# Eighteen of the last network's gate and up tile pairs as block products with seven multiplications, one weight sum added by a DMA

## The reference

```python
def _swiglu(h, w_gate, w_up, w_down):
    return (jax.nn.silu(h @ w_gate) * (h @ w_up)) @ w_down
...
        h = _rmsnorm(x, norm2_g[i]) * (1.0 + sc2) + sh2
        x = x + g2 * _swiglu(h, ffn_w_gate[i], ffn_w_up[i], ffn_w_down[i])
```

## Time and profile before

| what | value |
|---|---|
| median of 3 runs (lowest, highest) | 2106.22 us (2105.19, 2109.66) |
| span of the profiled execution, first to last instruction | 2104.2 us |
| median less span: start and end around it | 2.0 us |
| mean granted TensorE clock | 0.999 |
| TensorE busy / VectorE / ScalarE / GpSimd | 2086.9 / 1250.6 / 804.6 / 308.7 us |
| the three lines of `product`, share of the chain that ended last | 28% each |
| DMA, mean | 116 GB/s |

### The profile page before, as it was taken

How to read it: one execution, slowest core, us unless ns; L and a number is a source line. 1 busy time by engine, 2 the same in 40 slices (tenths; PEclk the granted TensorE clock), 3 DMA queues, 4 the chain that set the end, 5 groups by cost and what they waited for, 6 DMA issues and landing times.

```text
span 2104.2 us, 28285 instructions
## 1 busy us (share of the span) xinstructions
PE 2086.9 (99%) x9912; PEld 1711.1 (81%) x9912; DVE 1250.6 (59%) x1832; ACT 804.6 (38%) x1234; POOL 308.7 (15%) x369
## 2 busy tenths in 40 slices
PE   9999999999999999999999999999999999999999
PEld 8888888887888888877767888888888888888887
DVE  7666544787676654466996676654465466333332
ACT  6222333567442223344565442223343234222222
POOL 0122400650212230024310212210000000000000
PEclk9999999999999999999999999999999999999999
DMA  5555333320345642323300346542333223222232
GB/s 194 180 193 198 94 110 110 119 95 2 110 164 187 199 136 83 96 95 116 104 29 1 110 153 197 188 144 80 96 103 109 92 90 100 100 94 96 76 96 87
DMA packets 79573, 243.33 MB, mean 116 GB/s; under 512 B 12784, under 2 KB 13424, under 8 KB 79376
## 3 DMA queue, kind: packets, MB, share of 16 engines
q1 hardware_dynamic: 61376, 189.61, 27.7%
q0 software_dynamic: 18128, 52.84, 8.1%
HBM read 235.84 MB, written 2.29 MB: 113 GB/s over the span
## 4 chain that ended last, share of the span: by engine, by line
PE 92%; DVE 6%; ACT 1%; issue 1%; DMA 0%; SPq 0%; ACTq 0%; DVEq 0%
PE ps L738 28%; PE ps L740 28%; PE ps L739 28%; PE ps L1050 2%; DVE ps L2048 1%; PE ps L1032 1%; PE ps L1011 1%; DVE tmp L1692 1%; DVE small L1946 1%; PE ps L1174 0%; DVE ropA L1919 0%; DVE qA L1921 0%; PE ps L1014 0%; DVE score L2157 0%; PE ps L769 0%
## 5 line engine op out<-in xcount | busy, mean ns | idle before, releaser
L738 PE MATMUL ps<-h_hi,w_hi 128*128 128x512 f32 x1888 | 740.1, 392 | 2.4 <-issue 1.1
L740 PE MATMUL ps<-h_hi,w_lo 128*128 128x512 f32 x1888 | 735.0, 389 | 0.0
L739 PE MATMUL ps<-h_lo,w_hi 128*128 128x512 f32 x1888 | 734.7, 389 | 0.0
L1649 DVE TENSOR_TENSOR w_lo<-w_raw,w_hi 128x1024 fp32r<-128x1024 f32 x336 | 411.6, 1226 | 383.9 <-ACT w_hi L1257 369.5
L1257 ACT ACTIVATE w_hi<-w_raw 128x1024 fp32r<-128x1024 f32 x383 | 402.4, 1052 | 242.5 <-PE ps L740 240.7
L738 PEld LDWEIGHTS ps<-h_hi,w_hi 128*128 128x128 f32 x1888 | 353.6, 187 | 83.3 <-issue 8.4
L740 PEld LDWEIGHTS ps<-h_hi,w_lo 128*128 128x128 f32 x1888 | 353.6, 187 | 75.3
L739 PEld LDWEIGHTS ps<-h_lo,w_hi 128*128 128x128 f32 x1888 | 353.7, 187 | 72.9 <-issue 0.2
L738 PE MATMUL ps<-hid_hi,w_hi 128*128 128x512 f32 x704 | 273.9, 389 | 0.0
L739 PE MATMUL ps<-hid_lo,w_hi 128*128 128x512 f32 x704 | 273.9, 389 | 0.0
L740 PE MATMUL ps<-hid_hi,w_lo 128*128 128x512 f32 x704 | 273.9, 389 | 0.0
(11 more groups left out here) (321 smaller groups left out, 1794.5 us busy)
## 6 DMA issues: line engine op xcount, KB each, us to landing
ada_raw<-in_ada_w POOLq DMA_DIRECT2D x96, 512.0 KB, 4.8
w_raw<-in_gate SPq DMA_DIRECT2D x88, 512.0 KB, 3.5
w_raw<-in_up SPq DMA_DIRECT2D x88, 512.0 KB, 3.2
w_raw<-in_down SPq DMA_DIRECT2D x64, 384.0 KB, 3.1
w_raw<-in_down SPq DMA_DIRECT2D x64, 320.0 KB, 2.9
w_raw<-in_w_mix_c SPq DMA_DIRECT2D x24, 512.0 KB, 3.2
w_raw<-in_w_mix_b SPq DMA_DIRECT2D x17, 512.0 KB, 3.4
w_raw<-in_w_mix SPq DMA_DIRECT2D x16, 512.0 KB, 3.2
```

The lines of the kernel that those rows point to most:

```text
L738: pe.matmul(dest, s_hi, m_hi, start=first and n == 0, stop=False)
L739: pe.matmul(dest, s_hi, m_lo, start=False, stop=False)
L740: mm = pe.matmul(dest, s_lo, m_hi, start=False, stop=last and n == len(pairs) - 1)
L1649: dve.tensor_tensor(chunk(w_lo, slot, WT), chunk(w_raw, slot, WT), f32(chunk(w_hi, slot, WT)), ALU.subtract).then_inc(w_lo_done, 1)
```

## The change

In the last network (`SEVEN = (3,)`) the tile pairs 4 to 21 (`UNIT0 = 4`, 18 units) are no longer two products over 8 chunks of 512 tokens. The gate and up tile of a pair, and the two halves of the contraction, form a 2x2 block matrix; the two halves of the features of h and the two halves of the tokens form another. Their product is made with seven block multiplications (A11, A12, S2, S1, S3, S4, A22), each over 4 chunks with 256 tokens. For that it adds:

- on the activations, once: four sums for each of 4 chunk pairs (`t_sums`, VectorE), their high parts (`t_high`, ScalarE) and low parts (`t_low`, VectorE), in `t_hi` and `t_lo`, which lie under chunks of `hid_hi`
- on the weights, for each pair: S3 = gate's first half + up's first half (`third_sum`); S1 = up's first half + up's second half, which GpSimd adds by a DMA with `accum_op` from DRAM into the raw slot (`first_sum`); S2 from gate's first half and S1 (`second_sum`); S4 from gate's second half and S2 (`fourth_sum`); then high and low parts of all
- on the results: ScalarE copies four partial products out of PSUM (`keep_part`), VectorE adds (L2190, L2197) and multiplies (L2205) into `hid_whole`, which lies under `hid_lo`
- high and low parts of hidden tiles 5 to 21 move from the loop to the first turn of `down`, which takes its two output tiles part by part in turn (`by_parts`).

The diff, cut to its core:

```diff
+        _, t_hi, t_lo = stage_memory([("under_t", 6 * T, F32), ("t_hi", 8 * T, F32R), ("t_lo", 8 * T, F32R)])
+        _, hid_whole = stage_memory([("under_hid", FC * T, F32), ("hid_whole", FC * T, F32)])
+        _, t_sum, h_whole = stage_memory([("under_sums", (FC + 10) * T, F32), ("t_sum", 4 * T, F32), ("h_whole", KC * T, F32)])
...
+        UNIT0 = 4
+        UNITS = FC - UNIT0
+        SEVEN = (3,)
+        PART = {"A11": 1, "A12": 2, "S2": 3, "S1": 4, "S3": 5}
+        KEPT = {"A11": 1, "S2": 2, "S1": 3, "S3": 4}
+        W_SUM = {"S3": 1, "S2": 2, "S4": 3}
...
+            def first_sum(n, u, i):
+                pool.wait_ge(w_sum_done, i * 6 + (3 * nth_unit(n, u) + W_SUM["S3"]))
+                pool.dma_start(raw_half(n, u, 2), A[f"up{n}"][bass.ds(i * 2 + u, 1), :, HW:WT].rearrange("a p n -> (a p) n"),
+                               accum_op=ALU.add).then_inc(first_sum_in, 16)
+            with pool.Fori(0, UNITS // 2) as i:
+                for e in range(2):
+                    first_sum(3, UNIT0 + e, i)
 
...
+                def half_product(dest, name, moving_of, first, last):
+                    at = half_of(n, name)
+                    for c in range(KC // 2):
+                        cut = slice(at + c * P, at + (c + 1) * P)
+                        m_hi, m_lo = moving_of(c)
+                        pe.matmul(dest, w_hi[:, cut], m_hi, start=first and c == 0, stop=False, skip_group_check=not first)
+                        pe.matmul(dest, w_hi[:, cut], m_lo, start=False, stop=False, skip_group_check=not first)
+                        mm = pe.matmul(dest, w_lo[:, cut], m_hi, start=False, stop=c == KC // 2 - 1, skip_group_check=not first)
+                    return mm
...
+                def unit(i, e):
+                    u = UNIT0 + e
+                    m, F, g = nth_unit(n, u), n * FC + u, unit_job(n, u)
+                    a, b, c = (unit_bank(u, what) for what in "abc")
+                    pe.wait_ge(hid_done, i * 2 + (F + 1))
+                    pe.wait_ge(first_lo_done, i * 2 + (m + 1))
+                    half_product(a, "A11", h_moving(0, 0), True, False).then_inc(part_done, 1)
+                    half_product(b, "A12", h_moving(1, 0), True, True).then_inc(part_done, 1)
+                    pe.wait_ge(w_lo_done, i * 4 + (g + 1 + RING))
+                    pe.wait_ge(part_kept, i * 8 + (4 * m + KEPT["A11"]))
+                    half_product(a, "S2", t_moving(1), False, False).then_inc(part_done, 1)
+                    pe.wait_ge(w_lo_done, i * 4 + (g + 2 + RING))
+                    half_product(c, "S1", t_moving(0), True, False).then_inc(part_done, 1)
+                    pe.wait_ge(third_lo_done, i * 2 + (m + 1))
+                    pe.wait_ge(part_kept, i * 8 + (4 * m + KEPT["S2"]))
+                    half_product(a, "S3", t_moving(2), False, False).then_inc(part_done, 1)
+                    pe.wait_ge(part_kept, i * 8 + (4 * m + KEPT["S1"]))
+                    half_product(c, "S4", h_moving(1, 1), False, True).then_inc(job_done, 1)
+                    pe.wait_ge(part_kept, i * 8 + (4 * m + KEPT["S3"]))
+                    half_product(a, "A22", t_moving(3), False, True).then_inc(job_done, 1)
+                def down(i, by_parts=False):
                     for s in range(8):
-                        tile, part = s // 4, s % 4
+                        tile, part = (s % 2, s // 2) if by_parts else (s // 4, s % 4)
...
+                    up(1)
+                    pe.wait_ge(t_lo_done, KC // 2 * (SEVEN.index(n) + 1))
+                    with pe.Fori(0, UNITS // 2) as i:
+                        for e in range(2):
+                            unit(i, e)
+                    down(0, True)
...
+                def first_high_of(u, i, e):
+                    raw_arrived(act, n, u, i, 0)
+                    if u == UNIT0 and e is None:
+                        act.wait_ge(job_done, unit_job(n, u) + 1)
+                    else:
+                        act.wait_ge(part_done, i * 10 + (5 * nth_unit(n, u - 1) + PART["A12"]))
+                    at = half_of(n, "A11")
+                    act.activation(w_hi[:, at:at + WT], w_raw[:, (unit_job(n, u) % RING) * WT:(unit_job(n, u) % RING + 1) * WT],
+                                   ACT.Copy).then_inc(first_hi_done, 1)
...
+                def second_high_of(u, i, which):
+                    if which:
+                        act.wait_ge(first_sum_in, i * 32 + 16 * (nth_unit(n, u) + 1))
+                    else:
+                        act.wait_ge(w_sum_done, i * 6 + (3 * nth_unit(n, u) + W_SUM["S4"]))
+                    act.wait_ge(job_done, i * 4 + (unit_job(n, u - 1) + 1 + which + RING))
+                    at, slot = half_of(n, ("S2", "S1")[which]), (unit_job(n, u) + which) % RING
+                    act.activation(w_hi[:, at:at + WT], w_raw[:, slot * WT:(slot + 1) * WT], ACT.Copy).then_inc(w_hi_done, 1)
...
+                def unit(i, e, last=False):
+                    u = UNIT0 + e
+                    v = u + 1
+                    keep_part(i, u, "A11")
+                    if last:
+                        hidden_high(UNIT0)
+                        early_down(0)
+                    else:
+                        first_high_of(v, i, e)
+                    keep_part(i, u, "S2")
+                    keep_part(i, u, "S1")
+                    keep_part(i, u, "S3")
+                    if last:
+                        early_down(1)
+                        early_down(2)
+                    else:
+                        third_high_of(v, i, e)
+                        second_high_of(v, i, 0)
+                    act.wait_ge(gate_sum_done, i * 2 + (nth_unit(n, u) + 1))
+                    act.activation(gate_sum(u), gate_sum(u), ACT.Silu).then_inc(silu_done, 1)
+                    if not last:
+                        second_high_of(v, i, 1)
+                def early_down(s):
...
+                def t_sums(k):
+                    first, near, far = 4 * (KC // 2 * SEVEN.index(n) + k), chunk(h_whole, k), chunk(h_whole, k + KC // 2)
+                    low, up_shift = slice(0, HT), shift[:, k + KC // 2:k + KC // 2 + 1]
+                    high = slice(HT, T)
+                    dve.tensor_tensor(t_room(k, 0), near[:, high], near[:, low], ALU.subtract).then_inc(t_sum_done, 1)
+                    dve.scalar_tensor_tensor(t_room(k, 2), near[:, high], shift_gap[:, k:k + 1], far[:, high],
+                                             ALU.add, ALU.subtract).then_inc(t_sum_done, 1)
+                    dve.wait_ge(t_sum_done, first + 1)
+                    dve.scalar_tensor_tensor(t_room(k, 1), far[:, high], up_shift, t_room(k, 0),
+                                             ALU.add, ALU.subtract).then_inc(t_sum_done, 1)
+                    dve.wait_ge(t_sum_done, first + 3)
+                    dve.scalar_tensor_tensor(t_room(k, 3), far[:, low], up_shift, t_room(k, 1),
+                                             ALU.add, ALU.subtract).then_inc(t_sum_done, 1)
...
+                def third_sum(u, i):
+                    raw_arrived(dve, n, u, i, 0)
+                    raw_arrived(dve, n, u, i, 1)
+                    dve.tensor_tensor(sum_room(n), raw_half(n, u, 0), raw_half(n, u, 2), ALU.add).then_inc(w_sum_done, 1)
+                def second_sum(u, i):
+                    dve.wait_ge(first_lo_done, i * 2 + (nth_unit(n, u) + 1))
+                    dve.wait_ge(first_sum_in, i * 32 + 16 * (nth_unit(n, u) + 1))
+                    dve.tensor_tensor(raw_half(n, u, 0), raw_half(n, u, 0), raw_half(n, u, 2), ALU.add).then_inc(w_sum_done, 1)
+                def fourth_sum(u, i):
+                    dve.wait_ge(w_sum_done, i * 6 + (3 * nth_unit(n, u) + W_SUM["S2"]))
+                    dve.tensor_tensor(raw_half(n, u, 1), raw_half(n, u, 1), raw_half(n, u, 0), ALU.add).then_inc(w_sum_done, 1)
+                def first_low_of(u, i):
...
+                def unit(i, e, last=False):
+                    u = UNIT0 + e
+                    v, m = u + 1, nth_unit(n, u)
+                    if last:
+                        whole_low(UNIT0)
+                        split(J + UP_JOBS)
+                    else:
+                        third_sum(v, i)
+                        first_low_of(v, i)
+                        second_sum(v, i)
+                        fourth_sum(v, i)
+                    dve.wait_ge(part_kept, i * 8 + (4 * m + KEPT["S3"]))
+                    dve.tensor_tensor(unit_bank(u, "e"), kept_part(u, "S3"), kept_part(u, "S1"), ALU.add).then_inc(up_sum_done, 1)
+                    if last:
+                        split(J + UP_JOBS + 1)
+                    else:
+                        third_low_of(v, i)
+                    dve.wait_ge(job_done, i * 4 + (unit_job(n, u) + 1 + RING))
+                    both = gate_sum(u).rearrange("p (h t) -> p h t", h=2)
+                    dve.tensor_tensor(both, both, gate_banks(u), ALU.add).then_inc(gate_sum_done, 1)
+                    if last:
```

(45 more changed lines are left out.)

213 lines of the change are left out of this document (192 added, 21 removed).

## The result

The changed kernel takes **2141.83 us** (median of 4 runs, 2138.63 to 2144.38) against 2106.06 of the kernel before in the same runs: 1.0165 of its time, 95% interval 1.0153 to 1.0178. I had forecast 2117 us. Slower was right and 2142 lies in the range, but the loss is 35.8 us and not 10.8, and that is the miss to be explained. On the profiled executions it is 2138.4 - 2104.2 = 34.2 us.

What follows compares the result with a forecast made beforehand. TensorE was taken to bound the kernel now. First unit +6.2, 17 units 0, down +3.7 and clock +0.9 give +10.8 us on a 2104.2 us span; with 2.0 outside the span, 2117 us, range 2099 to 2143.

Steps and rivals of the forecast that it cites:

- L: Time of GpSimd's adding DMA from issue to landing in the loop, taken as 4.0 us, upper bound 5.9.
- The bound at the bottom: Lower limit of 2.8 us for the adding DMA, 2.0 + 0.76, as if adding were free and queues empty.
- the 3.8 us row: Trace row of a 256 KB GpSimd transfer with one SP load beside it, 3.8 us from issue to use.
- the ring: In the loop, third sum, adding DMA, second sum and VectorE's remaining in-order work wait on each other; period 10.88 us.
- The handover of 0.30: Time from the end of VectorE's third sum to GpSimd's start on the adding DMA, 0.30 us.
- The period, 6.88 + L: Loop time per unit: 5.83 from second to next third sum, 1.05 for third sum and handovers, plus the DMA's time.
- the ring hides a slower clock: Claim that a slower TensorE clock after the first unit's stalls costs nothing, since the loop's closed chain of waits covers it.
- The clock behind it: Slower TensorE clock after the stall ahead of down, bounds 0 and 1.7 us, half taken: +0.9.
- rival 4: Weight loads in the loop don't overlap, 188 ns each, 15.8 us a unit: +88, 2194 us; chance 0.02.
- Rival 2: Adding slow in the DMA engines or waiting behind SP's load: 5.5 us to landing, +37.8, 2144 us; chance 0.19.
- Rival 1: TensorE stays the loop's bound, the adding DMA at or under 3.1 us: -5.1, 2101 us; chance 0.2.
- My estimate of 3.6 by that rule: Adding DMA's time with empty queues if adding only doubles the source reads: 2.8 + 0.76 = 3.6 us.

Runs made afterwards that it cites:

- run 1: Changed kernel with VectorE's third weight sum made one unit earlier, the adding DMA kept: 2110.04 us, 1.0014 of the kernel before.

## Why the prediction was right in its sign and wrong in its size

**The step that failed is L**, put as "Half of the excess over 2.8 for that: 2.8 + 0.76 + 0.5 = 4.0". Term by term:

| | forecast | measured |
|---|---|---|
| plain transfer, nothing beside it | 2.8 | 2.9 (one issue) |
| adding | +0.76 | +1.0 in the loop, +1.1 to 1.3 with nothing beside it |
| the up load beside it | +0.5 | +1.0 (5.0 against 4.0 with the load held); +0.8 to 1.0 against the first units |
| L | 4.0 | 5.0 |

The bound at the bottom was good. The adding came 0.24 us or more above my 0.76: I had a second pass of the data and no longer issue. The larger part of the miss is the load, which I halved. I had argued that the data of the two "overlap for a part, less than in the 3.8 us row". That row's excess over 2.8 is 1.0 us, and the load takes the whole of it here too: its issue comes 1.2 us **ahead** of the adding one, and 0.24 us behind in that row. The run with the load held gives 4.0 with the adding in it, so holding it takes away exactly this 1.0. And the load is not there by chance: VectorE's last low part of a unit sets it free, the same part that stands in front of the third sum (SP issues at 1881.33, the third sum begins at 1881.21). It was in the ring: I gave it a half in L and put "the SP loads" at nothing otherwise.

**The handover of 0.30** was the second slip, 0.66 measured: I took it from another GpSimd DMA. With GpSimd's loop written out it is 0.30 here too. Its worth of 18 x 0.36 shows only with the load out of the way.

**The period, 6.88 + L**: from second sum to next third sum 5.74 us for my 5.83. With 5.0 and 0.66 in it 6.88 + 0.36 - 0.09 + 5.0 = 12.15, as measured. So the ring itself, its members and its closing, was right, and the loss is my own function of L with 1.0 and 0.36 too little.

The balance in spans: the first unit ended at 1804.92 for my 1802.6, +2.3. The 17 others took 2008.79 - 1804.92 = 203.9, 11.99 each for my 10.88: **+18.9**. (That is less than 12.15 because the second unit made up for the lateness of the first; my "the ring hides a slower clock" held in that way.) Down 3.92 us for 3.7, +0.2. The clock behind it: 11 matmuls at 0.427 for 0.227, 2.2 us for my 0.9, +1.3; the granted clock had fallen to 0.50, that is 1.2 GHz, after TensorE stood from 2008.8 on. 10.8 + 22.7 = 33.5 of the 34.2 us.

**Right:** TensorE's pitch, 0.120 us in the runs without the wait and a unit of 10.08 for my 10.0, so rival 4 (weight loads that don't overlap) is out. The third sum of the first unit at 1784.09 for 1784.3, the second at 1789.80 for 1789.35. VectorE's waits, 18 of them at the named line, 4.5 us each for 3.2, too short by L and the handover. **Off:** TensorE's stops in the loop are mostly 1.5 to 2.0 us, not 0.9, and are ended by ScalarE's kept part, not by VectorE's low part. That was on my list of what would show me wrong, and it did: a copy of 1024 columns (L1530, 1891.15 to 1892.19) stands ahead of the kept part in ScalarE's queue. It places the stop and doesn't make it, since run 1 has none. The stop in the first unit was 6.99 us and not 4.4, though it ended at 1796.10 where I had 1796.85: it stood ahead of the third product, where I had it ahead of the fourth. So five products were left and not four, 1.4 us more, and the granted clock had fallen in the stop as well (0.50 and 0.60 in the 4 us behind it): they took 8.82 us for my 5.72.

**Rival 2** (L = 5.5, 2144 us) came nearest, and for the second of its two reasons, "or waits behind SP's load". It named the larger cause and had 0.19. Rival 1's 2101 us is what the loop does once the wait is gone.

The page "Collectives: The Full Stack" of the Trainium skill (Part 3, "The bandwidth ceiling") says that the add itself costs no cycles, only a second source read, which halves the rate. The trace agrees in so far as the adding transfer fills the DMA engines for twice the time of the plain one (1.74 and 0.88 us); whether that is the second read or the arithmetic, no run tells. The issue on GpSimd, 0.33 us longer, is on top. My estimate of 3.6 by that rule, with empty queues, stands against 4.0 to 4.2 in the first units and 4.0 in the loop with the load held. On the page "DMA: Bandwidth & Descriptors" (section "Anatomy of one DMA — SWDGE (gpsimd) path") of the Trainium skill a GpSimd transfer is put at 2.0 us plus its bytes at 436 GB/s, 2.6 us for these 256 KB, an estimate from that page; the plain one alone took 2.9.
